# Three calls moved within their engines' queues, in a four-layer model kernel on one core

## The reference

```
first_block:   for layer 0:  x += g * even_mixer(adaln(x));  x += g * swiglu(adaln(x))
               for layer 1:  x += g * s5_mixer(adaln(x));    x += g * moe_swiglu(adaln(x))
               x = rmsnorm(x)
second_block:  for layer 0:  x += swiglu/2;  x += ssd_mixer(rmsnorm(x));                x += swiglu/2;  gated projection
               for layer 1:  x += swiglu/2;  x += neighbourhood_attention(rmsnorm(x));  x += swiglu/2;  gated projection
```

```
adaln(c, w, b):   shift, scale, gate = split(silu(c) @ w + b, 3)       # one row vector times (1024, 3072)
                  h = rmsnorm(x) * (1 + scale) + shift
even_mixer(h):    fq, fk, fv, ff, gq, gk, gv, gg, glr = split(h @ w_in)
                  fox = softmax(fq fk' / 8 + cum_t - cum_s, causal) fv           # 8 heads
                  gla: A[t, s] = sum_d q[t,d] k[s,d] exp(b[t,d] - b[s,d]),  s <= t,  b = cumsum(log_a)
                       o = A v, normed per head, times silu(gg)
                  return concat(fox, gla) @ w_o
neighbourhood_attention(h):  q, k, v = split(h @ w_qkv);  q, k = rmsnorm per head
                             softmax(q k' + bias) v, then @ w_out
```

## Time and profile before

| | us |
|---|---|
| median of 3 runs | 2923.7 |
| lowest, highest | 2922.91, 2931.41 |
| the profiled execution | 2931.41 |
| its span in the trace | 2929.7 |
| PE busy | 2813.6 (96%) |
| DVE busy | 1948.7 (67%) |
| ACT busy | 1403.2 (48%) |
| POOL busy | 277.0 (9%) |
| mean granted TensorE clock | 0.975 |

### The profile page before, as it was taken

How to read it: one execution, slowest core, us unless ns; L and a number is a source line. 1 busy time by engine, 2 the same in 40 slices (tenths; PEclk the granted TensorE clock), 3 DMA queues, 4 the chain that set the end, 5 groups by cost and what they waited for, 6 DMA issues and landing times.

```text
span 2929.7 us, 39664 instructions
## 1 busy us (share of the span) xinstructions
PE 2813.6 (96%) x15582; PEld 2440.7 (83%) x15583; DVE 1948.7 (67%) x2308; ACT 1403.2 (48%) x1568; POOL 277.0 (9%) x248
## 2 busy tenths in 40 slices
PE   6989999989999999999998999999999999998999
PEld 5868988877888888887877888888888988996888
DVE  5585453647888888887454763785477577585775
ACT  2223422216767776775433552343555455435554
POOL 0004851400000000000001000002100010020000
PEclk8969999999999999999999999999999999999999
DMA  8855564267999999997552563433356456572553
GB/s 262 273 175 162 178 211 131 89 230 256 336 346 366 335 341 356 357 339 278 185 203 87 192 199 119 140 115 115 116 188 221 140 167 200 165 205 69 182 184 112
DMA packets 504828, 609.70 MB, mean 208 GB/s; under 512 B 50201, under 2 KB 371836, under 8 KB 504700
## 3 DMA queue, kind: packets, MB, share of 16 engines
q1 hardware_dynamic: 502224, 606.82, 62.3%
q10 hardware_dynamic: 2476, 1.06, 0.1%
HBM read 605.75 MB, written 1.05 MB: 207 GB/s over the span
## 4 chain that ended last, share of the span: by engine, by line
PE 80%; DVE 7%; DMA 4%; POOL 3%; issue 3%; ACT 3%; SPq 0%; DVEq 0%; ACTq 0%; POOLq 0%
PE bank L1450 13%; PE bank L2038 7%; PE bank L1454 7%; PE bank L1442 7%; PE bank L1267 4%; PE bank L1884 4%; PE bank L1888 4%; PE bank L1897 4%; PE bank L1797 3%; PE bank L1319 3%; PE bank L1946 2%; DMA ring<-in_o_exp_down 2%; PE bank L1937 2%; PE bank L1938 2%; PE bank L1802 1%
## 5 line engine op out<-in xcount | busy, mean ns | idle before, releaser
L3287 DVE TENSOR_TENSOR ring_r<-ring,store_area_r 128x2048 fp32r<-128x2048 f32 (+1 forms) x344 | 809.1, 2380 | 200.4 <-ACT store_area_r L2449 197.4
L2449 ACT ACTIVATE store_area_r<-ring 128x2048 fp32r<-128x2048 f32 (+1 forms) x344 | 670.7, 1974 | 229.0 <-PE bank L1454 57.2
L1450 PE MATMUL bank<-hT_sq_r,store_area_r 128*128 128x512 f32 x1376 | 347.2, 394 | 0.6 <-DVE ring_r L3287 0.6
L1450 PEld LDWEIGHTS bank<-hT_sq_r,store_area_r 128*128 128x128 f32 x1376 | 249.0, 190 | 45.7 <-DVE ring_r L3287 0.9
L2038 PE MATMUL bank<-hT,ring 128*128 128x256 f32 x1024 | 229.9, 380 | 0.0
L3743 DVE TENSOR_TENSOR ring_r<-ring,store_area_r 128x3072 fp32r<-128x3072 f32 x64 | 195.0, 3087 | 49.2 <-ACT store_area_r L2882 49.1
L2038 PEld LDWEIGHTS bank<-hT,ring 128*128 128x128 f32 x1024 | 190.8, 190 | 27.0 <-issue 3.1
L1454 PEld LDWEIGHTS bank<-hT_sq_r,ring_r 128*128 128x128 f32 x1376 | 188.0, 191 | 13.5
L2882 ACT ACTIVATE store_area_r<-ring 128x3072 fp32r<-128x3072 f32 x64 | 163.5, 2561 | 73.7 <-DMA ring<-in_o_exp_down 58.0
L1454 PE MATMUL bank<-hT_sq_r,ring_r 128*128 128x256 f32 x1376 | 192.0, 282 | 0.0
L1193 POOL TENSOR_TENSOR silu_g<-silu_g 128x768 f32<-128x768 f32 (+2 forms) x14 | 29.9, 2136 | 1708.4 <-ACT silu_g L2461 1337.9
(11 more groups left out here) (560 smaller groups left out, 4800.8 us busy)
## 6 DMA issues: line engine op xcount, KB each, us to landing
ring<-in_o_exp_gate SPq DMA_DIRECT2D x88, 1024.0 KB, 7.1
ring<-in_o_exp_up SPq DMA_DIRECT2D x88, 1024.0 KB, 7.3
ring<-in_ffn_w_gu SPq DMA_DIRECT2D x88, 1024.0 KB, 6.9
ring<-in_o_exp_down SPq DMA_DIRECT2D x32, 1536.0 KB, 8.8
ring<-in_ffn_w_down SPq DMA_DIRECT2D x32, 1408.0 KB, 8.7
ring<-in_o_exp_down SPq DMA_DIRECT2D x32, 1280.0 KB, 11.6
ring<-in_ssd_w_in SPq DMA_DIRECT2D x32, 1024.0 KB, 7.1
ring<-in_e_mod_mix_w SPq DMA_DIRECT2D x12, 1024.0 KB, 8.7
```

The source lines that it names most:

```text
L1450: mm(bank[:, :], w_hi(k), x_both(k), start=(start and k == blocks[0]), stop=False)
L2449: activation(dst, slot(u, s, kk), ACT.Copy).then_inc(w_high, 1)
L3287: nc.vector.tensor_tensor(slot(u, s, kk, rounded=True), slot(u, s, kk), as_f(high), ALU.subtract).then_inc(w_low, 1)
```

## The change

Three calls, each on a straight queue, stand at another place; no instruction is added or taken away, and no operand differs. On ScalarE in `na()`, `raw_root("mix_1")` comes ahead of `high(1)`. On VectorE in the key loop of `even_mixer`, `raw(i + 3)` follows `key(i)` for i = 0 to 4, where `raw(i + 2)` followed it for i = 1 to 5. On VectorE in `out_product("even_out")`, `products_in_place` follows the two `even_low` calls.

```diff
@@ -2993,8 +2993,8 @@
                 se.wait_ge(unit_done, Unit(first).at(-1))
                 high(0)
                 raw_inputs("mix_1")
+                raw_root("mix_1")
                 high(1)
-                raw_root("mix_1")
                 se.wait_ge(unit_done, Unit(first).at(1))
                 high(2)
                 se.wait_ge(factor_cols, 1)
@@ -3490,8 +3490,8 @@
                 tally.wait(ve)
                 for i in range(NB):
                     key(i)
-                    if i >= 1 and i + 2 < NB:
-                        raw(i + 2)
+                    if i + 3 < NB:
+                        raw(i + 3)
                 ve.wait_ge(key_used, NB)
                 for hd in range(4):
                     nc.vector.tensor_tensor(gla_a[:, hd, :], banks[hd][:, 0:3 * P], upper[:, :, :].rearrange("p a t -> p (a t)"),
@@ -4089,9 +4089,9 @@
                         first_low("ffn2_1")
                         inputs_low("ffn2_1", 0, X_HEAD["ffn2_1"])
                     if stage == "even_out" and i == 0:
-                        products_in_place(Unit(base[stage] + 2), mod_count(OUT_MOD))
                         for s in range(2):
                             even_low(0, s)
+                        products_in_place(Unit(base[stage] + 2), mod_count(OUT_MOD))
                 if stage == "even_out":
                     u = Unit(base[stage] + 2)
                     mod_out(u, OUT_MOD, banks[2 * u.r])
```

## The result

The changed kernel takes 2948.89 us (median of 4 runs, 2945.54 to 2950.28), the kernel before 2927.55 beside it (4 runs, 2922.91 to 2932.06): ratio 1.0068, 95% interval 1.0056 to 1.0082. That is some 20 us slower (16 to 24). The forecast was 18.8. The profiled execution took 2949.95 us, its span is 2948.2, 18.5 more than the one before.

The account below looks back on a forecast made before the run. The prediction took TensorE, 80% of the chain with hardly any slack, to bound the kernel. Its terms 5.1 + 7.1 + 6.6 = 18.8 us on the median 2923.7 gave 2942.5, range 2934 to 2950.

Parts of the forecast that it names:

- Key loop: Key loop: each raw waits for the products of the key just issued, the loop turns serial up to block 5; costs 5.1 us.
- a small one half of that, 0.88: Key loop: at half clock a large block's product takes 1.77 us, a small block's half of that, 0.88.
- cost of 1.9: Key loop: with a full clock throughout, the products would end at 154.8, a cost of 1.9 us.
- Output projection: Output projection: VectorE idles for the high parts, products end 5.3 us late, clock adds 1.8; costs 7.1 us.
- The 1.8 for each hole: Output projection and attention entry: the lower clock behind each TensorE hole adds 1.8 us.
- The bound of 8.1: Output projection: upper bound, 5.3 us of delay plus 2.8 for the clock at worst.
- Attention entry: Attention entry: high(1) queued behind the waiting root leaves TensorE a 4.8 us hole, clock adds 1.8; costs 6.6 us.
- Rule and row: Both holes: time lost is half the time at 1.2 GHz; slow stretches of 6 us cost 3.0 each, sum 21.2.
- A: Rival, all three places: one stall is swallowed later, 2934 to 2938 us; chance 0.15 together with D.
- B: Rival, whole kernel: not slower, existing slow-clock stretches go and give back 8.0 us, 2927.7; chance 0.08.
- C: Rival: 6 us slow stretches behind both holes, or slow products behind the mask for longer; 21 to 26 us; chance 0.14.
- D: Rival, key loop: the edit does nothing, the earlier raw finds TensorE's products done; 13.7 us, 2937.4; chance 0.15 with A.

Follow-up runs that it names:

- key_four: Changed key-loop order, other two places as in the kernel before, plus a fourth place for the key buffer: ratio 1.0005.
- only_key: Kernel before with only the key loop's edit: ratio 1.0017.
- key_fill: Kernel before with the key loop's edit and float32 products that nobody reads where TensorE waits there: ratio 1.0036, median 2938.36 us.
- clock_fill_short: Kernel before, order untouched, with products that nobody reads at five places where the clock falls: ratio 0.9990, 2923.5 us against 2927.43.
- out_fill: Kernel before with the output projection's edit and 20 float32 products that nobody reads ahead of TensorE's wait there: ratio 1.0041.
- attn_fill: Kernel before with the attention entry's edit and 36 products that nobody reads where TensorE would idle there: ratio 1.0022.
- attn_sum_early: Attention entry as changed, but TensorE forms the sum of squares after unit 0's first slot, against the kernel before: ratio 1.0005.
- attn_half: Kernel before with half of the attention entry's edit, the root between the two high parts of unit 1: ratio 0.9998.
- only_attn: Kernel before with only the attention entry's edit: ratio 1.0023.
- out_between: Kernel before with the output projection's low parts among the products, one after the sixth, one after the seventh: ratio 1.0010.
- only_out: Kernel before with only the output projection's edit: ratio 1.0019.

## Why the prediction held, and where its terms were off

The direction, the places and the passing of each delay were right. The sum came near, 18.8 against 18.5 in the spans and about 20 in the runs, but partly because errors offset each other: the three places cost 20.75, every term was too small, and the 18.5 of the spans is lower only because the untouched stretches happened to be 2.25 shorter.

The time itself, 2948.89, lies in the stated range of 2934 to 2950, but above the inner one, 2938 to 2945, to which the forecast gave 0.60. Part of that is the base: the forecast stood on a median of three runs, 2923.7, while the kernel before has medians of 2927.4 to 2928.9 in all later groups of its runs. The other part is the terms below.

- **Key loop, 5.1 forecast, 6.5 measured.** The mechanism is as told, and `key_four` shows it. The step that was mis-sized is "a small one half of that, 0.88": I took throughput, 7.06 / 4 / 2, for a step that now begins and ends with a hand-over. It takes 1.08 at half clock, the large step 1.96 and not 1.77. Also the clock was down at product 0 already, which took 1.08 and not 0.65 (in `only_key` 0.64, and key to mask was 17.38). With the durations of `key_fill` at full clock (0.64, 1.10, 48 records 2.89), the same serial loop would take 1.22 + 1.53 + 2 x 1.67 + 2.40 + 1.31 + 2.89, about 12.7 us, so half clock costs the new order some 5. That is not to be set against 11.30, as the forecast's "cost of 1.9" at full clock did: the old order ran at half clock too. With the clock at 1.00 from 140 to 148 and 0.60 from 148 to 151 (`clock_fill_short`) the old order took 10.40 with four added products in it, so the turns themselves cost 2.3 us or more, and the rest of the 6.5 is the half clock that they are taken at. That split is an estimate, not run.
- **Output projection, 7.1 forecast, 7.2 measured.** Two errors cancel. VectorE's delay was 4.3 and not 5.3: the products took 6.1 us behind the low parts, not 6.56, the second high part was ready 9.5 us behind the additions, not 9.8, and from there to the first product it was 2.2 us, not 2.45. The clock cost 2.9 and not 1.8. (The 1.8 for each hole was high by its own row, which gives 15.74 - 14.08 = 1.66, and still too low here.) From the second additions to the root 7.76 us, against 4.83 before, and `out_fill` shows 4.55 and 7.51 for the 24 records at the two clocks. The bound of 8.1 holds.
- **Attention entry, 6.6 forecast, 7.0 measured.** The hole is 4.78, forecast 4.8; the clock 2.2, forecast 1.8. `attn_fill` takes the second part away but for 0.2 us, `attn_sum_early` and `attn_half` both.
- **Rule and row.** Half of the time at the lower clock gave 21.2 for two slow stretches of 6 us. The three places came to 20.75, but with a larger key term, so this sum doesn't decide for it. At each place by itself the rule can be read. At the output projection the clock was 0.50 from the start of the modulation's sum at 252.79 to 256 and, at 0.77, for 2.8 of 256 to 262, 6.0 us in all, and 2.9 to 3.0 were lost. At the attention entry with 2.2 us lost the slow stretch should be 4.5 us. The windows give 3.0 from 2580 to 2583 and, at 0.74, 3.6 of 2583 to 2590, less the piece before 2582.12 in which nothing ran: about 4.5. That rule is the Trainium skill's, page "TensorE: Matmul & The Clock Gate", section "HAM oscillation — how this bites in real kernels"; the trace agrees with it at both places.
- **Rivals.** A (absorbed) fell with the single edits. B (the clock gives it back) fell too. Some slow stretches did go: the output projection's 64 records took 15.52 and not 16.91, and those of the state-space layer 14.05 and not 15.74. But that isn't the edits' doing, since kernels with the same code there show both values (15.61 in `only_attn` and 16.91 in `attn_half`, 14.05 in `key_four` and 15.74 in `only_key`), and two slow stretches were added. `clock_fill_short` shows what could be had from the clock at these places in the old order, about 5 us in its trace, its fastest run, not 8. C was half right, and the measured 2948.89 lies in its 2945 to 2950: the slow stretch of 6 us came behind the hole at the output projection, at a price of 2.9, but was 4.5 us long at the attention entry. The forecast had given C 0.14. D fell: `raw` waited for TensorE ahead of each of its five pairs.
- **What it says of the edits.** Each put a call that waits ahead of one that had been free to run, on a queue whose next reader is TensorE. In the kernel before, the same calls ran inside the wait.

## What to carry to other kernels

Before moving a call on an in-order engine, ask what its wait ends on, and what behind it could have run meanwhile. In `attn_half` and `out_between` the order was free as long as the first piece that TensorE needs came out in time; where it did not, as in `only_attn`, the hole was paid in full and the clock's share on top. A buffer's depth is part of the order: "one ahead" in a ring of three means waiting on the reader of the block just made, and a fourth place makes the same order harmless. When a pipelined loop becomes serial, price its steps from hand-over to hand-over, not by throughput, and add what the granted clock does to a sparse TensorE.

## What was not expected of the hardware

The untouched stretch from the norm's root to the attention entry took 2306.6 us before, 2304.8 after, 2303.3 in `only_key`, 2303.4 in `only_out` and 2299.6 in `only_attn`, with the same instructions. Of the 7 us between the first and the last, 4 lie between 1384 us of the span and the next layer's first sum (227.0 and 223.0), where the granted clock of the first 116 us was 0.97 in one and 1.00 in the other: behind a wait of the same length (2.84 and 2.85 us) the same 16 products took 6.78 us before and 3.91 in `only_attn`. This scatter is as large as one edit's loss, and it is why the local distances carry the verdicts here (at the second and third place they repeat within 0.1 us in all kernels with the old code, and within 0.6 with the changed one, added products aside) and the whole times only confirm them.
